# Moving the last head's walk of an RWKV scan out of the scan stage and into the finishing stage

## What is computed

```python
def _wkv_step(S, inp):
    r_t, w_t, k_t, v_t, a_t, b_t = inp
    sa = jnp.einsum('zbhvk,zbhk->zbhv', S, a_t)
    S = S * w_t[..., None, :] + sa[..., :, None] * b_t[..., None, :] + v_t[..., :, None] * k_t[..., None, :]
    return S, jnp.einsum('zbhvk,zbhk->zbhv', S, r_t)

def rwkv_out(y, h, xx, r, k_mod, v, mu, ln_g, ln_b, r_k, g1, g2, wo):
    y = layernorm(y, ln_g.reshape(RWKV_HEADS, RWKV_HEAD), ln_b.reshape(RWKV_HEADS, RWKV_HEAD), GN_EPS)
    bonus = jnp.einsum('bthk,zbthk->bth', _heads(r) * r_k, _heads(k_mod))
    y = y.astype(r.dtype) + bonus[..., None] * _heads(v)
    gate = jax.nn.sigmoid((h + xx * mu[5]) @ g1) @ g2
    return (y.reshape(bsz, n, d) * gate) @ wo

x = x + gt1 * yl                                  # yl = rwkv_out(...)
hl2 = rmsnorm_2(x, norm2_g[i]) * (1 + sc2) + sh2  # then the router's logits, and the experts
```

## Time and profile before

| | us |
|---|---|
| median of 3 runs | 4310.55 (4308.35 to 4314.49) |
| the profiled execution | 4311.74 |
| its span | 4309.8 |
| last head's walk alone, about | 3609.0 to 3636.4 |
| finishing stage, first DVE work to the router's first operation | 3636.7 to 3738.0 |

### The profile page before, as it was taken

How to read it: one execution, slowest core, us unless ns; L and a number is a source line. 1 busy time by engine, 2 the same in 40 slices (tenths; PEclk the granted TensorE clock), 3 DMA queues, 4 the chain that set the end, 5 groups by cost and what they waited for, 6 DMA issues and landing times. The chain is left out here.

```text
span 4309.8 us, 78120 instructions
## 1 busy us (share of the span) xinstructions
PE 3577.5 (83%) x31346; PEld 2528.0 (59%) x31346; DVE 2089.9 (48%) x3273; ACT 1244.6 (29%) x2681; POOL 1369.2 (32%) x1069
## 2 busy tenths in 40 slices
PE   8889999998999999968787848876888887587874
PEld 6667777556778887752222326635888886432221
DVE  4559963448983455640000036625878875400002
ACT  3352223443223223321111021223454443111112
POOL 4444453343443554720000023403455452000001
PEclk9999999999999999979898978997999997798997
DMA  4125532214542223449999963334223223599997
GB/s 125 47 79 178 182 133 79 63 50 150 181 161 76 98 74 120 146 179 420 421 421 421 421 244 108 125 134 130 67 64 78 53 78 113 210 394 426 426 426 298
DMA packets 245738, 819.09 MB, mean 190 GB/s; under 512 B 61336, under 2 KB 68840, under 8 KB 185680
## 3 DMA queue, kind: packets, MB, share of 16 engines
q1 hardware_dynamic: 236960, 786.13, 48.8%
q0 software_dynamic: 7920, 28.84, 1.7%
q10 hardware_dynamic: 576, 0.09, 0.0%
HBM read 738.84 MB, written 76.12 MB: 189 GB/s over the span
## 5 line engine op out<-in xcount | busy, mean ns | idle before, releaser
L2810 POOL DMA_INDIRECT moe0e_xg<-moe_h,moe_first_rows x19 | 18.0, 950 | 593.7 <-DMA moe_first_rows<-moe_table 544.0
L3758 PE MATMUL scan_bank<-scan_T,scan_off 64*64 64x64 f32 x3840 | 163.0, 223 | 43.5 <-issue 35.9
L1209 DVE SCALAR_TENSOR_TENSOR f0u_ada<-hT,condition,f0u_ada 128x512 f32<-128x512 f32 x168 | 196.9, 1242 | 0.2 <-DVE f0u_ada L1209 0.2
L1209 DVE SCALAR_TENSOR_TENSOR f1u_ada<-hT,condition,f1u_ada 128x512 f32<-128x512 f32 x168 | 191.2, 1207 | 0.2 <-DVE f1u_ada L1209 0.2
L2842 PE MATMUL moe0e_p_g<-moe_ring,moe0e_xT 128*64 128x512 f32 x608 | 175.1, 652 | 18.2 <-ACT moe0e_xT L2880 9.7
L2810 POOL DMA_INDIRECT moe1e_xg<-moe_h,moe_first_rows x16 | 15.1, 942 | 537.0 <-DMA moe_first_rows<-moe_table 454.9
L3482 POOL TENSOR_TENSOR scan_off<-scan_pairs,scan_join 128x256 f32<-128x256 f32 x240 | 181.3, 795 | 0.0
L359 POOL TENSOR_TENSOR gmi_w_lo<-gmi_rows_w,gmi_w_hi 128x512 fp32r<-128x512 f32 x64 | 120.5, 1883 | 161.6 <-ACT gmi_w_hi L399 161.6
L3758 PEld LDWEIGHTS scan_bank<-scan_T,scan_off 64*64 64x64 f32 x3840 | 140.2, 138 | 51.8 <-issue 42.8
L2842 PE MATMUL moe0e_p_u<-moe_ring,moe0e_xT 128*64 128x512 f32 x608 | 169.1, 631 | 0.0
L359 POOL TENSOR_TENSOR p_w_lo<-p_rows_w,p_w_hi 128x512 fp32r<-128x512 f32 (+3 forms) x88 | 113.4, 1290 | 163.0 <-ACT p_w_hi L399 163.0
(11 more groups left out here) (745 smaller groups left out, 10403.5 us busy)
## 6 DMA issues: line engine op xcount, KB each, us to landing
moe_ring<-in_moe_w_gu_dram SPq DMA_DIRECT2D x280, 1024.0 KB, 20.9
moe_ring<-in_moe_w_down_dram SPq DMA_DIRECT2D x140, 1024.0 KB, 22.6
hT<-in_ada_w_dram SPq DMA_DIRECT2D x48, 1024.0 KB, 6.6
f0u_w<-in_ffn_w_gate_up_dram SPq DMA_DIRECT2D x22, 1024.0 KB, 4.9
f1u_w<-in_ffn_w_gate_up_dram SPq DMA_DIRECT2D x22, 1024.0 KB, 4.8
gmi_rows_w<-in_ga_w_in_dram SPq DMA_DIRECT2D x64, 256.0 KB, 2.8
gmo_w<-in_ga_w_out_dram SPq DMA_DIRECT2D x64, 256.0 KB, 3.0
p_rows_w<-in_ab_w_in_dram SPq DMA_DIRECT2D x48, 256.0 KB, 2.7
```

The source lines that it names most:

```text
L1209: ins = V.scalar_tensor_tensor(out=acc[:, z, :], in0=src, scalar=cond[:, n * HALF + k, z:z + 1], in1=acc[:, z, :], op0=ALU.mult, op1=ALU.add)
L2810: pool.indirect_dma_start(xg[:], None, H.h, bass.IndirectOffsetOnAxis(rows[:, 0:1], 0)).then_inc(gathered, 16)
L3758: mm = nc.tensor.matmul(out[r], lhsT[r], rhs[r], start=start, stop=stop, skip_group_check=True)
```

## The change

The walk of the last head leaves `rwkv_scan`. Its buffers and its eight semaphores are made outside both stages (`LastWalk`, at the other end of the memory), and `walk_finish` replaces `mixer_finish`: it holds the walk of head 15 on TensorE and ACT, and DVE normalises and joins the first 896 columns (14 heads) of the tiles beside it. The last 128 columns (heads 14 and 15) are joined for all four tiles at once when the walk is done. TensorE's projection products all stand behind the walk's last step; the k-slice of the last 128 columns comes by itself. All logits stand behind all products. There is one PSUM bank for turning where there were two.

In the scan, the rounding `scan_w_hi` on ACT moves from the end of a head to just behind the walk's steps 0 and 1, and on POOL `scan_eed` (`diagonals`) goes behind `scan_w_lo` and the shift's add.

```diff
@@ rwkv_scan, gpsimd
                     nc.gpsimd.tensor_tensor(kh[:], cs(km), cs(e_neg), ALU.mult).then_inc(s["kh_made"], 1)
+
+                def diagonals(h):
                     pool.wait_ge(s["bd_ready"], h + 1)
...
                     if ahead is not None:
                         factors(ahead)
+                    split_block(h)
+                    if h:
+                        add_shift(h - 1)
+                    if ahead is not None:
+                        diagonals(ahead)
+
+                def split_block(h):
                     pool.wait_ge(s["hi_made"], h + 1)
                     nc.gpsimd.tensor_tensor(w_lo[:], w_raw[:], w_hi[:], ALU.subtract).then_inc(s["lo_made"], 1)
-                    if h:
-                        add_shift(h - 1)
@@ rwkv_scan, scalar
                     walk_both(0)
                     walk_both(1)
+                    act.wait_ge(s["raw_loaded"], 32 * h + 32)
+                    act.wait_ge(s["w_stored"], 32 * h)
+                    A(w_hi[:], w_raw[:], ACT.Copy).then_inc(s["hi_made"], 1)
                     copy_turned(0)
...
-                        if n == NZ - 4:
-                            act.wait_ge(s["raw_loaded"], 32 * h + 32)
-                            act.wait_ge(s["w_stored"], 32 * h)
-                            A(w_hi[:], w_raw[:], ACT.Copy).then_inc(s["hi_made"], 1)
...
-                for j in range(STEPS):
-                    walk_x(LAST, j)
-                    walk_sa(LAST, j)
-                    walk_sm(LAST, j)
-                walk_x(LAST, STEPS)
@@ walk_finish, tensor
+                for j in range(STEPS):
+                    for part in (walk_state, walk_solve, walk_share):
+                        part(j)
+                        if j == 6 and part is not walk_state:
+                            turn_o(0, 0 if part is walk_solve else 1)
+                for do, what in between:
+                    do(*what)
+                turn_o(2, 0)
+                turn_o(2, 1)
+                for k in range(KD - 1):
+                    for h in range(2):
+                        products(2, k, h)
+                turn_last()
+                for t in range(3):
+                    for h in range(2):
+                        products(t, KD - 1, h)
+                turn_o(3, 0)
+                turn_o(3, 1)
...
                 for t in range(NT):
...
+                    turn_xn(t)
+                    logit(t)
@@ walk_finish, scalar
+                ASIDE = {1: (square, 0), 2: (square, 1), 3: (invert, 0), 8: (square, 2), 9: (invert, 1)}
                 nc.scalar.preload_act_table_set("natural_log_exp_and_others")
...
+                for j in range(STEPS):
+                    walk_x(j)
+                    walk_sa(j)
+                    if j == 6:
+                        round_o(0, 0)
+                    if j < STEPS - 1:
+                        walk_sm(j)
+                    if j == 6:
+                        round_o(0, 1)
+                    if j in ASIDE:
+                        do, t = ASIDE[j]
+                        do(t)
```

More of the change, by code:

```diff
@@ L3965, in mixer_finish, with walk_finish @@
+def walk_finish(nc, name, S, a, walk, y, bonus, gate, wo, x_tiles, mods, R, H):
+    halves = [slice(0, BANK), slice(BANK, D)]
+    lat = SEQ // CH
+    lo, hi = slice(0, HK), slice(HK, P)
+    EARLY = D - P
+    early, last = slice(0, EARLY), slice(EARLY, D)
+    NE, LAST = EARLY // HK, HEADS - 1
+    K7 = NT
+    TURNS = [(0, 0), (0, 1), (1, 0), (1, 1), (2, 0), (2, 1), (K7, 0), (3, 0), (3, 1)]
     with Stage(nc, name) as st:
         gain, row = st.sb("gain", [P, D]), st.sb("row", [P, D])
-        g = [st.sb(f"gate{t}", [P, D]) for t in range(NT)]
+        g = [st.sb(f"gate{u}", [P, EARLY]) for u in range(2)]
@@ new lines, in _ @@
+                for do, what in between:
[11 more added lines that the diff above has]
+                turn_o(3, 1)
+                for k in range(KD):
+                    for h in range(2):
+                        products(3, k, h)
@@ new lines, in round_o, with join_last @@
+                def round_o(t, h):
+                    act.wait_ge(turned, order(t, h))
+                    if t >= 2:
+                        act.wait_ge(walked_products, t - 1)
+                    n = len(blocks(h))
+                    A(x_hi[t % 2][:, 4 * h:4 * h + n, :], tr[:, 0:n, :], ACT.Copy).then_inc(hi_made, 1)
+                def join_last():
+                    act.wait_ge(last_step, LAST_CENTRED)
+                    A(sq_last, y[:, :, last], ACT.Square).then_inc(last_step, 1)
+                    act.wait_ge(last_step, LAST_VAR)
+                    A(ln_var_l, var_l, ACT.Ln, scale=1.0 / HK, bias=S.eps[:, 2:3]).then_inc(last_step, 1)
+                    act.wait_ge(last_step, LAST_LN)
+                    A(rstd_l, ln_var_l, ACT.Exp, scale=-0.5).then_inc(last_step, 1)
@@ L4106, in invert_x, with round_last @@
+                def round_last():
+                    act.wait_ge(turned, order(K7, 0))
+                    A(x7_hi[:], tr[:], ACT.Copy).then_inc(hi_made, 1)
                 def invert_x(t):
                     act.wait_ge(residual_made, t + 1)
[L4108 to L4109 removed]
@@ new lines, in join, with rest_o @@
+                    c.step(V.tensor_tensor(y[:, t, early], y[:, t, early], gain[:, early], ALU.mult))
+                    c.step(V.tensor_tensor(y[:, t, early], y[:, t, early], bonus[:, t, early], ALU.add))
+                    dve.wait_ge(gate_loaded[t % 2], 16 * (t // 2) + 16)
+                    V.tensor_tensor(y[:, t, early], y[:, t, early], g[t % 2][:], ALU.mult).then_inc(joined, 1)
+                def rest_o(t, h):
+                    n = len(blocks(h))
+                    dve.wait_ge(hi_made, order(t, h))
+                    V.tensor_tensor(x_lo[t % 2][:, 4 * h:4 * h + n, :], tr[:, 0:n, :], x_hi[t % 2][:, 4 * h:4 * h + n, :], ALU.subtract).then_inc(lo_made, 1)
@@ L4173, in residual, with rest_last @@
+                def rest_last():
+                    dve.wait_ge(hi_made, order(K7, 0))
+                    V.tensor_tensor(x7_lo[:], tr[:], x7_hi[:], ALU.subtract).then_inc(lo_made, 1)
                 def residual(t):
```

355 lines of the change are left out of this document (222 added, 133 removed).

## The result

The changed kernel takes 4320.2 us (median of 10 runs, 4315.8 to 4334.8) where the kernel before takes 4310.3 (median of 10 on the same chip): a ratio of 1.0028, with a 95% interval of 1.0018 to 1.0038. The forecast was 4324, with 4306 to 4339 as its range. The profiled execution took 4315.83, its span 4314.0.

The account below looks back on a forecast made before the run. One core runs stage after stage, so only scan and finish can change: +17 for the scan and -3.6 for the finish give +13.4, against the median 4310.55 thus 4324 us, range 4306 to 4339.

Parts of the forecast that it names:

- Scan, +17: Both scan orders together, all heads: 13 + 7 - 3 = +17 us, bounds 0 and 33.
- Part 1: Scan, early rounding on ACT: waits for late loads, stalls sum to 26 us, 0.9 a head won back, 13 us left.
- swallowed: Scan: bonus products get about 1 us back, but lose it where the early rounding's load ends last.
- Part 2, 7 us: Scan, POOL's new order: one or two dense DVE operations wait longer, 0.5 us a head, 7 us; bounds 0 and 15.
- the 15 us: Scan, POOL's order by the skill's exclusion rule alone: both POOL operations hold DVE once every head, about 15 us.
- Hand-over: Scan to finishing stage: last stores land 2.8 us after issue, plus 0.3 for stage change; new stage starts at T = 3609.0.
- Walk: Last head's walk in the new stage: y copied at T + 36.3 = 3645.3 against 3636.4, +8.9 us.
- Products and tail: Finish behind the walk: products, then 24 us tail; overlap brings 12.5 us, less 8.9 paid before it: -3.6 us.
- rival 1: Scan: weight split's early place costs 0 to 5 us, finish gains 3.6; about 4309 us, chance 0.20.
- Rival 2: Scan neutral or up to 10 us faster, finish wins 10; 4295 us; needs sooner shift landing; chance 0.12.

Follow-up runs that it names:

- x3: Changed kernel with ScalarE's late rounding and GpSimd's old order both put back, so only the finish is new; 4305.2 us, ratio 0.9986 to the kernel before.
- x2: Changed kernel with GpSimd's old order put back (diagonals before subtraction and shift add), early rounding kept; 4311.5 us, ratio 0.9999 to the kernel before.
- x9: Changed kernel, weight block loaded once so rounding waits for no load, high half stored early, GpSimd's old order; 4297.7 us, ratio 0.9974.
- x11: Changed kernel, weight block loaded once so rounding waits for no load, high half stored early, GpSimd's new order kept; 4301.2 us, ratio 0.9974.
- x5: Changed kernel with SyncE's stores and next head's loads moved ahead of its wait for the y copy; 4299.4 us, ratio 0.9970 to the kernel before.
- x12: The changed kernel itself, timed again beside other runs; 4323.1 us, ratio 1.0028 to the kernel before.
- x4: Kernel before with only the scan's two new orders (early rounding, GpSimd's order), old walk and finish; 4326.4 us, ratio 1.0033.
- x6: Changed kernel with the finishing stage's tail reordered and logits on two banks; 4317.9 us, ratio 1.0014 to the kernel before.
- x7: Changed kernel with both the early loads and stores and the reordered two-bank tail; 4288.5 us, ratio 0.9947 to the kernel before.
- x10: x7 with ScalarE's roundings of the last tile put ahead of its square of the first tile's residual; 4288.9 us, ratio 0.9948.

## Why the prediction was right, and which step was wrong

- **Scan, +17:** measured +16.9 in the profiled pair, 13.6 by the head table, and some 18 us by the ratios (changed against x3). The size was right, its making was not, so the hit on it is in part luck. Part 1's step "What it can win back is TensorE's and ACT's small waits between ... 0.7 a head" failed: I took the stall for a delay on the path, of which 0.9 us is won back. At the full clock a stall of up to 3 us is won back almost whole. What it costs is TensorE's clock, which I hadn't priced in the scan at all. The stall's own size, 26 us, is what x2 has with GpSimd's old order (25.6); the changed kernel has 42.7, because the bonus products' earlier end, which I called swallowed, lengthens the stall.
- **Part 2, 7 us:** the signs were seen (`scan_bh` 1.08 against 0.55, bonus products 0.96 against 1.85), but the sum shows as nothing (x9 against x11). The Trainium skill's rule in SBUF — State Buffer, section "Who interferes with whom", from which the 15 us came, agrees with the single operation; as a term of the sum it was wrong, since what the dense part takes, 0.8 us a head, the bonus products give back. What the order does cost comes through TensorE's clock: it lengthens part 1's stall, and it makes a second pause behind which the clock sometimes falls.
- **Hand-over:** forecast 3.2 us from the issue of the last store to the new stage; measured 3.0 (3612.66 to 3615.7). First X at T + 1.5.
- **Walk:** y copied forecast at T + 36.3, measured T + 35.7.
- **Products and tail:** last product forecast at T + 101.1, measured T + 100.2 (its start); last logit T + 125.1, measured T + 124.5; the tail 24.3 against a forecast of 24. Together -4.3 us, where -3.6 was forecast, and x3 alone -5 by medians.
- **Rivals:** rival 1 (the early place is hidden) is close to what x2 is, though its loads don't land in time; it came out at 4311.5, where 4309 was worked out. Rival 2 needed the loads to land sooner; x5 made them, and got 4299.4.

## What to carry to other kernels

Price a stall by what the engine behind it loses in clock, not only by the path: look at TensorE's granted clock in windows of 1 us around the place where it will wait. Here 14 of 16 heads with a stall under 2 us kept the full clock, and none of 14 with over 4 us did. When work moves forward in a queue, move its loads and stores too: a load that is issued behind the last thing of the head before is late for anything at the next head's front. Moving one block of SyncE's code turned a loss of 0.28% into a gain of 0.30%, and a tail with two banks made it 0.53%.

## What was not expected of the hardware

- In this scan of small 64x64 products a pause of TensorE of 3.0 us was followed by some 3 us at half its clock (0.50 from 3161.7 to 3165.1), and so was one of 1.3 us (0.50 from 3060.0 to 3061.0 in the windows above), but the short one in only 25 of 117 heads.
- The executions of one kernel tend to differ with this clock. In x12, the six with the lowest mean clock (0.907 and up) average 4325.1 us, the other six (up to 0.915) 4320.0; in x4 it is 4334.3 and 4322.8. In x6, x7, x9 and x10 the two hardly go together (correlation -0.1 to -0.2), so this is a tendency and not shown to be the cause.
